# dt's softplus chain of the Mamba-2 mixer from VectorE to GpSimd, its reciprocal as a squared power, and the sums by rank in three later iterations

## The reference, cut to what matters

```
proj = h @ w_in
z, xbc, dt = split(proj)                      # 2048, 4096 and 32 columns
xbc = silu(causal_depthwise_conv(xbc, conv_w, conv_b))    # 4 taps
dt  = softplus(dt + dt_bias)                  # 256 tokens x 32 heads
a   = -exp(a_log)
acs = cumsum(dt * a)                          # per head, along the tokens
decay = exp(acs[l] - acs[s])  for s <= l
y = (C B^T * decay) @ (x * dt)  + d_skip * x
```

## Time and profile before

| | |
|---|---|
| median of 3 runs | 1828.56 us (1826.66 to 1832.51) |
| profiled execution | 1827.93 us |
| its span, first to last instruction | 1826.2 us |
| PE busy | 1751.2 us, 96% of the span |
| DVE busy | 1233.4 us, 68% |
| ACT busy | 868.4 us, 48% |
| POOL busy | 70.8 us, 4% |
| mean granted TensorE clock | 0.982 of full speed |

### The profile page before, as it was taken

The page is one execution under the profiler, slowest core; times in us unless marked ns, Lnnn a source line. Parts: engine busy times, 40 slices in busy tenths (PEclk is TensorE's granted clock), DMA queues, the critical chain, the costliest instruction groups (busy, mean ns, idle before and its releaser), DMA issues.

```text
span 1826.2 us, 24702 instructions
## 1 busy us (share of the span) xinstructions
PE 1751.2 (96%) x9513; PEld 1505.2 (82%) x9513; DVE 1233.4 (68%) x1418; ACT 868.4 (48%) x1056; POOL 70.8 (4%) x122
## 2 busy tenths in 40 slices
PE   7999999989999999998899999999998899989998
PEld 6888889878888888887678888987886687878887
DVE  5666798665766677667657676875657474567676
ACT  5444565755444444446444444755345434445443
POOL 0000001120000000002000000001000000000000
PEclk9999999989999999999799999999999899999999
DMA  6655455324655565544216654554552265436552
GB/s 223 198 185 197 141 176 169 108 88 139 207 186 195 170 200 191 184 152 167 69 47 209 198 191 154 185 184 138 185 185 70 92 208 161 162 115 230 196 184 92
DMA packets 213089, 298.26 MB, mean 163 GB/s; under 512 B 12374, under 2 KB 168603, under 8 KB 213019
## 3 DMA queue, kind: packets, MB, share of 16 engines
q1 hardware_dynamic: 213018, 297.30, 49.8%
HBM read 296.21 MB, written 1.05 MB: 163 GB/s over the span
## 4 chain that ended last, share of the span: by engine, by line
PE 87%; DVE 6%; ACT 4%; issue 2%; DMA 1%; POOL 1%; SPq 0%; DVEq 0%; POOLq 0%; ACTq 0%
PE PS L437 26%; PE PS L443 13%; PE PS L338 11%; PE PS L339 11%; PE PS L393 7%; PE PS L357 4%; PE PS L428 2%; PE PS L429 2%; PE PS L430 2%; PE PS L332 1%; PE PS L334 1%; PE PS L333 1%; ACT whi L316 1%; DVE wlo L321 1%; PE PS L679 1%
## 5 line engine op out<-in xcount | busy, mean ns | idle before, releaser
L321 DVE TENSOR_TENSOR wlo<-raw,whi 128x2048 fp32r<-128x2048 f32 (+1 forms) x284 | 640.7, 2259 | 168.5 <-ACT whi L316 167.9
L316 ACT ACTIVATE whi<-raw 128x2048 fp32r<-128x2048 f32 (+1 forms) x284 | 536.3, 1890 | 438.4 <-PE PS L443 307.8
L437 PE MATMUL PS<-XT,whi 128*128 128x512 f32 x2016 | 506.8, 394 | 5.4 <-DVE XT L741 3.7
L437 PEld LDWEIGHTS PS<-XT,whi 128*128 128x128 f32 x2016 | 368.2, 190 | 75.1 <-issue 4.2
L443 PEld LDWEIGHTS PS<-XT,wlo 128*128 128x128 f32 x2016 | 274.2, 191 | 18.9
L443 PE MATMUL PS<-XT,wlo 128*128 128x256 f32 x2016 | 280.9, 283 | 0.0
L339 PE MATMUL PS<-whi,aT 128*128 128x512 f32 x400 | 156.3, 391 | 0.0
L338 PE MATMUL PS<-whi,aT 128*128 128x512 f32 x400 | 156.2, 390 | 0.0
L338 PE MATMUL PS<-whi,XT 128*128 128x512 f32 (+2 forms) x320 | 126.1, 395 | 1.2 <-ACT V L1914 1.1
L339 PE MATMUL PS<-whi,XT 128*128 128x512 f32 (+2 forms) x320 | 123.1, 386 | 0.0
L578 ACT ACTIVATE aT<-ff_a 128x512 fp32r<-128x512 f32 x50 | 31.6, 631 | 170.9 <-PE PS L393 162.5
(11 more groups left out here) (410 smaller groups left out, 2262.6 us busy)
## 6 DMA issues: line engine op xcount, KB each, us to landing
raw<-in_w_in SPq DMA_DIRECT2D x112, 512.0 KB, 4.5
raw<-in_ffn_w_gate SPq DMA_DIRECT2D x88, 512.0 KB, 4.5
raw<-in_ffn_w_up SPq DMA_DIRECT2D x88, 512.0 KB, 4.4
raw<-in_ffn_w_down SPq DMA_DIRECT2D x88, 512.0 KB, 4.1
raw<-in_ssm_w_in SPq DMA_DIRECT2D x48, 512.0 KB, 4.6
raw<-in_w_ffn_in SPq DMA_DIRECT2D x44, 512.0 KB, 4.2
raw<-in_w_ffn_out SPq DMA_DIRECT2D x22, 512.0 KB, 4.1
raw<-in_ssm_w_out SPq DMA_DIRECT2D x16, 512.0 KB, 4.4
```

The costliest lines, as they stand in the source:

```text
L316: act.activation(whi[s][:, 0:size], raw[s][:, 0:size], ACT.Copy).then_inc(hi_done, 1)
L321: dve.tensor_tensor(wlo[s][:, 0:size], raw[s][:, 0:size], whi[s][:, 0:size].bitcast(FP32), ALU.subtract).then_inc(lo_done, 1)
L437: return pe.matmul(o, whi[n % SLOTS][:, sl], XT[:, k, :, :].rearrange("p a n -> p (a n)"), start=(k == 0), stop=False)
```

## The change

GpSimd takes over `dt_quotient` and `dt_value`, at the head of `ssm_pool`. The reciprocal becomes a power of -0.5 and a square, since the same second operand (`neghalf`, a column of -0.5) is there already; the fused forms become single ones, so eight instructions of VectorE turn into eleven of GpSimd. A new semaphore `dt` tells VectorE that dt is there. VectorE makes the running sum behind the taps of block 4, the high sums by rank behind block 6 and the low ones behind block 8. `dta` counts these three; TensorE's transposes still wait for the first, and `scores(0)` waits for the third.

```diff
@@ scores(g), g == 0
                     pe.wait_ge(A["masked"], 1)
+                    pe.wait_ge(A["dta"], 3)
                     pe.wait_ge(A["tap"], 16)
@@ ssm_dve
-            def dt_quotient():
-                dve.wait_ge(A["e"], 2)
-                own.link(dve.tensor_scalar(hrow[:, H_D, :], hrow[:, H_E, :], 1.0, -1.0, ALU.add, ALU.add))
-                own.link(dve.tensor_scalar(hrow[:, H_Q, :], hrow[:, H_D, :], 1e-30, None, ALU.max))
-                own.link(dve.reciprocal(hrow[:, H_Q, :], hrow[:, H_Q, :]))
-                own.link(dve.tensor_tensor(hrow[:, H_Q, :], hrow[:, H_Q, :], hrow[:, H_E, :], ALU.mult))
-
-            def dt_value():
...
             def decay_sums():
+                dve.wait_ge(A["dt"], 1)
                 own.link(dve.tensor_scalar(hrow[:, H_DA, :], hrow[:, H_DT, :], expa[:, 0:1], -1.0, ALU.mult, ALU.mult))
-                own.link(dve.tensor_tensor_scan(out=hrow[:, H_ACS, :], data0=ones[0:H, :], data1=hrow[:, H_DA, :],
-                                                initial=0.0, op0=ALU.mult, op1=ALU.add))
+                dve.tensor_tensor_scan(out=hrow[:, H_ACS, :], data0=ones[0:H, :], data1=hrow[:, H_DA, :],
+                                       initial=0.0, op0=ALU.mult, op1=ALU.add).then_inc(A["dta"], 1)
+
+            def sums_hi():
+                dve.wait_ge(A["dta"], 1)
                 for r in range(SSM_R):
                     m = dve.tensor_scalar(by_rank[0:H, r, :], hrow[:, H_ACS, :], of_rank[:, r:r + 1], None, ALU.mult)
-                own.link(m)
+                m.then_inc(A["dta"], 1)
+
+            def sums_lo():
+                dve.wait_ge(A["dta"], 2)
                 for r in range(SSM_R):
...
-                if i == 1:
-                    dt_quotient()
-                if i == 2:
-                    dt_value()
-                if i == 3:
+                if i == 4:
                     decay_sums()
+                if i == 6:
+                    sums_hi()
+                if i == 8:
+                    sums_lo()
@@ ssm_pool
+            def dt_quotient():
+                pool.wait_ge(A["e"], 2)
+                own.link(pool.tensor_scalar(hrow[:, H_D, :], hrow[:, H_E, :], 1.0, -1.0, ALU.add, ALU.add))
+                own.link(pool.tensor_scalar(hrow[:, H_Q, :], hrow[:, H_D, :], 1e-30, None, ALU.max))
+                own.link(pool.tensor_tensor(hrow[:, H_Q, :], hrow[:, H_Q, :],
+                                            neghalf[0:SSM_HEADS, 0:1].to_broadcast([SSM_HEADS, SEQ]), ALU.pow))
+                own.link(pool.tensor_tensor(hrow[:, H_Q, :], hrow[:, H_Q, :], hrow[:, H_Q, :], ALU.mult))
+                own.link(pool.tensor_tensor(hrow[:, H_Q, :], hrow[:, H_E, :], hrow[:, H_Q, :], ALU.mult))
+                own.mark(pool.tensor_scalar(hrow[:, H_D, :], hrow[:, H_D, :], 0.0, None, ALU.is_equal))
+                own.link(pool.tensor_scalar(hrow[:, H_X, :], hrow[:, H_X, :], 0.0, None, ALU.max))
+                own.link(pool.tensor_tensor(hrow[:, H_D, :], hrow[:, H_D, :], hrow[:, H_E, :], ALU.mult))
+
+            def dt_value():
+                pool.wait_ge(A["e"], 3)
+                own.link(pool.tensor_tensor(hrow[:, H_Q, :], hrow[:, H_Q, :], hrow[:, H_LN, :], ALU.mult))
+                own.link(pool.tensor_tensor(hrow[:, H_Q, :], hrow[:, H_Q, :], hrow[:, H_D, :], ALU.add))
+                pool.tensor_tensor(hrow[:, H_DT, :], hrow[:, H_X, :], hrow[:, H_Q, :], ALU.add).then_inc(A["dt"], 1)
+
+            dt_quotient()
+            dt_value()
             pool.wait_ge(A["in"], 48)
             pool.wait_ge(A["coln"], 1)
```

More of the change, by code:

```diff
@@ L884, in build @@
         ssm_ctx.close()
-        A = sems("ssm", "in xb e dta dtN coln acc tap silu turned nat z b masked e_done m dx y y_read yz sq var r gs "
+        A = sems("ssm", "in xb e dt dta dtN coln acc tap silu turned nat z b masked e_done m dx y y_read yz sq var r gs "
                         "gt gh gl")
@@ L1228, in ssm_dve, with ssm_pool @@
             lo_upto(dve, at, no + 8)
-        def ssm_pool(pool):
+        def ssm_pool(pool, own):
             def by_head(g, col):
@@ L2402, in _ @@
             norm_pool(pool, 1)
-            ssm_pool(pool)
+            ssm_pool(pool, own)
             norm_pool(pool, 2)
```

## The result

The changed kernel took 1852.70 us (median of 6 runs, 1850.34 to 1858.09), the kernel before beside it 1830.41 us (6 runs, 1826.24 to 1834.41). The ratio is 1.0128 with a 95% interval of 1.0109 to 1.0147. It is slower, by 22.3 us where 31.6 were forecast. The time lies inside the range, but the mechanism was not the forecast one: it was the rival in which the power is slow but holds nobody (1848 to 1853 us).

What follows compares the result with a forecast made beforehand. TensorE was taken as the bound (87% of the chain), waiting early in the mixer for VectorE. +35.2 - (23.2 - 19.6) = +31.6 us on 1827.93 gave 1859.5, with 0.6 for the median 1860 us; range 1846 to 1866.

Steps and rivals of the forecast that it cites:

- the rival in which the power is slow but holds nobody: VectorE runs on to its wait for dt, block 7 starts at 282.4; 1848 to 1853 us, chance 0.14.
- The gain removed from VectorE: Quotient, value and sums leave VectorE ahead of the low halves; block 7 would start 6.3 us earlier.
- The power's price: GpSimd's power on 256 columns takes 39.8 us, from 154 ns for each further column.
- Who is held by the power: VectorE's low half of block 4 waits for GpSimd's power until 274.7, so block 4 starts 35.2 us later.
- The wait for dt costs nothing: GpSimd's chain ends by 288.5, before VectorE has added the taps of block 4 by 291: no cost.
- low clock: TensorE runs at its lower clock after the long pause, a loss taken as 2.0 us.
- The tensor_scalar with two operations: In GpSimd's chain, a tensor_scalar was taken to cost 0.78 us for 256 columns.
- the forecast's own range: 1856 to 1862 us, with the power between 36 and 40 us and the clock's bounds.
- +31.6 us: Whole kernel slower by +35.2 - (23.2 - 19.6), from the late start of block 4 to block 7.
- The forecast's mechanism: The power holds VectorE's low half of block 4 to its end; the sign turns at a power of 8.9 us.

Runs made afterwards that it cites:

- experiment 1: Changed kernel with GpSimd's power of 32 x 256 values replaced by a product of the same inputs; 1824.64 us, 0.9965 against the kernel before.
- experiment 11: Kernel before with dt's whole chain kept on VectorE but later (iterations 4, 5, 6, 8, 10, transposes behind block 8); 1825.25 us, 0.9979.
- experiment 2: Kernel before with only the running sum and sums by rank moved to iterations 4, 6 and 8, dt's chain staying on VectorE; 1824.53 us, 0.9973.
- (5): Changed kernel with the power on the first 64 of 256 columns only; 1825.28 us, 0.9978 against the kernel before.
- experiment 4: Changed kernel with the power on the first 128 of 256 columns only; 1834.56 us, 1.0021 against the kernel before.
- (9): Changed kernel with the power cut into thirty linked instructions of 2 columns, 60 columns in all; 1842.12 us in one run.
- (8): Changed kernel with the power cut into sixteen linked instructions of 8 columns, 128 columns in all; 1845.54 us in one run.
- (6): Changed kernel with the whole power cut into four linked instructions of 64 columns; 1852.91 us in one run.
- experiment 10: Kernel before with dt's whole chain kept on VectorE but later (iterations 4, 6, 8, 10, 14, transposes behind block 10); 1824.15 us, 0.9961.
- 3: Changed kernel with 1 + e, its floor and a real reciprocal on VectorE, the chain's other eight instructions on GpSimd; 1825.91 us, 0.9973.

## Why the prediction was right in sign and wrong in mechanism

**The gain removed from VectorE: right.** 6.3 us were worked out; experiment 1 has 5.7 and experiment 11 has 5.6. It comes from VectorE's load in iterations 1 to 3, and 4.85 of the 5.7 are had by moving the sums alone (experiment 2); the prediction gave no such split.

**The power's price: right.** 39.8 us forecast, 41.16 measured. Two powers of the series, (41.16 - 20.75) / 128 = 0.159 us a column with 0.34 us at the start; 8 columns would be 1.62 and 64 columns 10.5, as measured (1.62, 10.51). The three lengths of the earlier trace rows gave 0.154: the slope held over a factor of 64 in length.

**Who is held by the power: the step that failed.** The prediction let the low half of block 4 wait to 274.7. That low half ran at 236.10 in 2.28 us. The step carried from products over to a power, and no row there has a power beside an instruction with two SBUF inputs. In these runs a product that has begun holds a low half to its end and a power never does (0.02 us at most), at 2 to 256 columns and on 32 or 128 partitions. Only the other direction is common to both: a power waits for a low half under way. Why a power holds nobody stays open. Beside the runs stands what the page SBUF — State Buffer of the Trainium skill says in its section Who interferes with whom, that the first to issue keeps the shared ports for the whole instruction. As the first, products agree (a low half of 3.75 us beside one) and the power does not (2.28 us inside 41.16); GpSimd's tensor_scalars were met as the second only, and agree (2.88 us instead of 0.84).

**"The wait for dt costs nothing": wrong by what followed.** With nobody held, TensorE ran out of blocks at 258.3 while dt came at 281.94. The rival had this sum nearly to the end (us):

| | rival | measured |
|---|---|---|
| power | 232.5 to 272.3 | 234.38 to 275.54 |
| dt ready | 278.9 | 281.94 |
| block 7 starts | 282.4 | 285.36 |
| low clock | 2.0 us | 2.3 us |

The 1.9 us at the start are L1239, which met the low half of block 3 (2.88 us); the price of the power adds 1.4. Low clock: from 285.36 to 290.7 a matmul came every 0.21 us instead of 0.12, 5.3 x (1 - 0.12 / 0.21) = 2.3 us. The sum closes on experiment 1: 241.48 + 24.82 + 1.64 + 2.3 = 270.2, and 270.08 were measured. The tensor_scalar with two operations cost 1.08 us where 0.78 were taken, those with one 0.84 to 0.86; that is hidden in the same sum. That the time fell inside the stated range is owed to this rival, for which the range was drawn wide and which had a chance of 0.14; the forecast's own range, 1856 to 1862, missed it, and its +31.6 us were 9.3 too many.

**What decides the sign.** These kernels differ in the power's length alone. All in us; the end of GpSimd's chain is counted from the start of the norm's power L791:

| power | chain ends | TensorE waits | mixer |
|---|---|---|---|
| 0.60 (exp. 1) | 38.8 | 0 | 241.48 |
| 10.54 (5) | 46.9 | 0 | 241.67 |
| 20.75 (4) | 55.0 | 4.5 + 1.8 | 249.35 |
| 27.5 (9) | 62.0 | 11.5 + 1.6 | 256.06 |
| 32.5 (8) | 66.9 | 16.4 + 1.6 | 261.49 |
| 41.16 (after) | 75.3 | 24.8 + 1.6 | 270.08 |
| 42.3 (6) | 76.8 | 26.3 + 1.6 | 271.53 |

Up to 46.9 delay is free (0.2 us), and from 55.0 on each microsecond costs (271.53 - 249.35) / (76.8 - 55.0) = 1.02 us. The mixer's 247.16 us of before lie 2.19 below experiment 4; if the line holds so far down, which no run shows, the sign turns at a power of 20.75 - 2.19 / 1.02 = 18.6 us. The forecast's mechanism had put that point at 8.9.

## What to carry to other kernels

Two engines that hold each other up with one kind of instruction need not do so with another: before a wait is priced on that, the very pair must be in a trace; where it is not, the case in which nobody is held needs as much weight as the other. Behind a wait stands the whole queue, so price a moved value by when its consumer's engine runs out of other work; up to that moment lateness is free, and from it on it counts in full plus the clock's return. And before work is handed to another engine, try it later on its own: here that gave the same gain without a second engine.

## What the runs showed of the hardware that was not expected

- On GpSimd a power costs about 0.16 us for each column, on 32 and on 128 partitions alike, against 0.60 us for a whole product of 256. It waits for a low half of VectorE that is under way, and lets a low half run once it has itself begun.
- A stretch that no change touches varied from one profiled run to another, and the clock with it. The latent attention, between two later norms, took in the kernel before:

```profile
824.53:954.69 130.16, 114.83 (x609) 95.91 (x607) 85.38 (x197) 67.48 (x138) 12.93 (x15) 0.90 0.30 100
```

and in experiment 10, whose profiled span (1827.2 us) is thereby longer than that of before although its median is 7 us lower:

```profile
820.74:956.05 135.31, 116.98 (x609) 97.18 (x607) 85.25 (x197) 67.22 (x138) 12.94 (x15) 0.87 0.28 96
```

In the profiled runs of the changed kernel and of experiments 1, 2, 3, 5 and 11 it was 130.11, 132.78, 130.12, 130.44, 133.45 and 132.84 us. Of all thirteen profiled runs, those with 130.0 to 130.5 us there had a granted clock (third from the end) of 0.88 to 0.90, and those with 132.8 to 135.4 us one of 0.86 to 0.88. Whether that hangs on the kernel or on the run stays open; it is why gains of 5 us were read at the landmark.
